# First mixer of a two-trunk transformer kernel: the order of attention and gated-recurrence work across steps, and the place of the modulation chunks in the load order

## The reference

```python
mix = concat([pool_mixer(p), gla_output(gla_bidir(...)), latent_attention(ql, k_all, v_all)]) @ w_out
x = x + ga1 * mix
x = x + ga2 * squared_relu_mlp(rmsnorm(x) * (1 + sc2) + sh2, w_up, w_down)
```

## Time and profile before

| | |
|---|---|
| median of 3 runs | 1920.18 us (1917.31 to 1926.2) |
| the profiled execution | 1921.07 us, its span 1919.3 us |
| PE busy | 1735.9 us, 90% |
| DVE busy | 1071.7 us, 56% |
| ACT busy | 704.2 us, 37% |
| mean granted PE clock | 0.942 |
| mixer of layer 0 | about 166.8 to 308.7 us from the start |
| mixer of layer 1 | about 847.1 to 936.5 us |

### The profile page before, as it was taken

How to read it: one execution, slowest core, us unless ns; L and a number is a source line. 1 busy time by engine, 2 the same in 40 slices (tenths; PEclk the granted TensorE clock), 3 DMA queues, 4 the chain that set the end, 5 groups by cost and what they waited for, 6 DMA issues and landing times.

```text
span 1919.3 us, 25681 instructions
## 1 busy us (share of the span) xinstructions
PE 1735.9 (90%) x10636; PEld 1399.4 (73%) x10636; DVE 1071.7 (56%) x1632; ACT 704.2 (37%) x878; POOL 81.6 (4%) x87
## 2 busy tenths in 40 slices
PE   5999888799999998988969996987999979779997
PEld 2886456677777777764669995675999766669996
DVE  2665545554444445764566775655666464566654
ACT  2423444321323123433444444363433343633332
POOL 0020000100000001100000001000000010010000
PEclk8999978899999999997889998988999989889999
DMA  9326860324344334258445555431654563335552
GB/s 340 117 103 218 284 224 1 134 87 151 133 150 149 140 132 145 94 208 313 169 143 201 190 180 170 178 132 45 197 176 165 180 225 122 122 110 176 176 174 90
DMA packets 172371, 309.18 MB, mean 161 GB/s; under 512 B 3264, under 2 KB 54720, under 8 KB 171616
## 3 DMA queue, kind: packets, MB, share of 16 engines
q1 hardware_dynamic: 168592, 293.98, 43.9%
q10 hardware_dynamic: 3376, 12.00, 1.8%
q0 software_dynamic: 288, 1.57, 0.2%
HBM read 305.44 MB, written 2.10 MB: 160 GB/s over the span
## 4 chain that ended last, share of the span: by engine, by line
PE 76%; DVE 11%; ACT 6%; DMA 4%; issue 2%; POOL 1%; DVEq 0%; ACTq 0%; POOLq 0%; SPq 0%
PE bank L581 58%; PE twin L581 15%; DVE ring_r L1230 3%; PE bank L590 3%; ACT arena L1961 2%; ACT arena_r L1961 2%; DMA ring<-in_w_in 2%; DMA ring<-in_w_mod 2%; DVE arena L1230 1%; POOL rs L2373 1%; DMA ring<-in_w_up 1%; DVE params L1230 1%; DVE arena L1314 1%; DVE arena_r L1230 1%; DVE X L1713 1%
## 5 line engine op out<-in xcount | busy, mean ns | idle before, releaser
L581 PE MATMUL bank<-arena_r 128*128 128x512 f32 (+2 forms) x2128 | 704.0, 377 | 15.4 <-DVE arena_r L1831 6.7
L1230 DVE TENSOR_TENSOR ring_r<-ring,arena_r 128x4096 fp32r<-128x4096 f32 (+4 forms) x96 | 393.9, 4103 | 236.2 <-ACT arena_r L1961 235.4
L581 PEld LDWEIGHTS bank<-arena_r 128*128 128x128 f32 x2128 | 406.6, 191 | 95.9 <-issue 8.0
L1961 ACT ACTIVATE arena_r<-ring 128x4096 fp32r<-128x4096 f32 (+4 forms) x96 | 323.4, 3369 | 393.9 <-DMA ring<-in_w_up 161.8
L581 PE MATMUL twin<-actT_r,arena_r 128*128 128x256 f32 x1408 | 255.3, 285 | 0.4 <-DVE actT_r L1230 0.4
L581 PE MATMUL bank<-ring_r,arena_r 128*128 128x512 f32 x624 | 246.7, 395 | 0.0
L581 PE MATMUL bank<-arena_r,actT_r 128*128 128x512 f32 (+3 forms) x624 | 219.5, 383 | 15.9 <-DVE params L1230 6.3
L581 PEld LDWEIGHTS twin<-actT_r,arena_r 128*128 128x128 f32 x1408 | 220.9, 193 | 1.0 <-DVE actT_r L1230 0.8
L1961 ACT ACTIVATE arena<-bank 128x512 f32<-128x512 f32 (+4 forms) x193 | 91.5, 474 | 343.6 <-PE bank L581 291.7
L581 PE MATMUL twin<-actT_r,ring_r 128*128 128x256 f32 x704 | 200.0, 284 | 0.0
L581 PE MATMUL bank<-ring_r,actT_r 128*128 128x512 f32 (+3 forms) x496 | 183.7, 370 | 0.0
(11 more groups left out here) (194 smaller groups left out, 1685.7 us busy)
## 6 DMA issues: line engine op xcount, KB each, us to landing
ring<-in_w_mod SPq DMA_DIRECT2D x24, 2048.0 KB, 8.8
ring<-in_w_ada SPq DMA_DIRECT2D x24, 2048.0 KB, 8.1
ring<-in_w_gate_up SPq DMA_DIRECT2D x44, 1024.0 KB, 7.7
ring<-in_w_down SPq DMA_DIRECT2D x20, 2048.0 KB, 8.0
ring<-in_w_up SPq DMA_DIRECT2D x16, 2048.0 KB, 7.9
ring<-in_w_in SPq DMA_DIRECT2D x12, 2048.0 KB, 9.2
ring<-in_w_out SPq DMA_DIRECT2D x8, 2048.0 KB, 8.6
ring<-in_w_down SPq DMA_DIRECT2D x8, 1792.0 KB, 7.5
```

Source lines behind the costliest of these rows:

```text
L581: ins = nc.tensor.matmul(out_, lhsT, rhs, start=start, stop=stop)
L1230: return v.tensor_tensor(o, x, y, op)
L1961: return nc.scalar.activation(o, x, func, **kw)
```

## The change

Load order: the last modulation chunk of each mixer moves ahead of out1 half 0, so the order is ..., mod, mod, out1 half 0, out1 half 1, up1 chunk 0, up1 chunk 1. Three places ahead of up1 chunk 0 now stands that modulation chunk, and three ahead of up1 chunk 1 stands out1 half 0.

Mixer: DVE takes the maxima of step i + 2 in step i instead of those of i + 1, and it does so behind `attended`, which now is for the pair that ended in step i - 2. PE makes its scores ahead of `turned1`. The parts of a gated tile are spread wider (PE: w, w + 1, w + 3, w + 5; DVE: w, w + 2, w + 4, w + 5). `WEIGHTED1` moves to 2, 6, 10, 14, so step w + 4 of a tile is step w of the next. ACT's block of gated exponentials is cut in two. The fills move up, all of them to the head of the step.

```diff
-        out += ins[:early] + [("par1", l, 0)] + ins[early:] + take(BESIDE1[l] - 1)
-        out += [("out1", l, 0)] + take(1) + [("out1", l, 1)]
+        out += ins[:early] + [("par1", l, 0)] + ins[early:] + take(BESIDE1[l])
+        out += [("out1", l, h) for h in range(2)]
...
-WEIGHTED1, FILLS1 = [[1, 6, 11, 16], [1, 7]], [(0, 1, 2, 3, 5, 6, 7, 9, 11, 12, 14, 16, 18, 20), (0, 1, 2, 4, 5, 6, 8, 9, 11, 13)]
-SUMS1, COLUMNS1, HALVES1 = [21, 7], [22, 13], [20, 12]
+WEIGHTED1 = [[2, 6, 10, 14], [2, 6]]
+FILLS1 = [(0, 1, 2, 3, 5, 6, 8, 9, 11, 12, 13, 15, 17, 19), (0, 1, 2, 4, 5, 6, 8, 9, 11, 13)]
+SUMS1, COLUMNS1, HALVES1 = [20, 7], [21, 13], [20, 12]
...
# PE
-                    if i in FILLS1[l] and i not in WEIGHTED1[l]:
+                    if i in FILLS1[l]:
                         fill()
+                    if i % 2 == 0 and i + 2 < n:
+                        scores1(l, i + 2)
                     if i < n:
                         turned1(l, i)
-                    if i % 2 == 0 and i + 2 < n:
-                        scores1(l, i + 2)
                     for p in ended(l, i - 1):
                         values1(l, p)
-                    if i in FILLS1[l] and i in WEIGHTED1[l]:
-                        fill()
                     for t in tiles:
                         w = WEIGHTED1[l][t]
-                        if i == w:
-                            if t + 1 in tiles:
-                                logs(l, t + 1)
+                        if i == w and t + 1 in tiles:
+                            logs(l, t + 1)
+                        if i == w + 1:
                             gated_scores(l, t)
-                        if i == w + 1:
+                        if i == w + 3:
                             gated_values(l, t)
-                        if i == w + 3:
+                        if i == w + 5:
                             gated_turned(l, t)
...
# DVE
                 largest1(l, 0)
+                largest1(l, 1)
                 differences(l, 0)
                 for i in range(n + 1):
-                    if i + 1 < n:
-                        largest1(l, i + 1)
+                    for p in ended(l, i - 2):
+                        attended(l, p)
+                    if i + 2 < n:
+                        largest1(l, i + 2)
+                    for p in ended(l, i):
+                        inverse_sums(l, p)
                     for t in tiles:
                         w = WEIGHTED1[l][t]
+                        if i == w + 2:
+                            masked(l, t)
+                        if i == w + 4:
+                            if t == 0:
+                                gate_values(l)
+                            gated_out(l, t)
+                        if i == w + 5:
+                            gated_norm(l, t)
                         if i == w:
                             ...
                             weighted(l, t)
-                        if i == w + 1:
-                            masked(l, t)
-                            if t + 1 in tiles:
-                                differences(l, t + 1)
-                        if i == w + 2:
-                            ...
-                            gated_out(l, t)
-                        if i == w + 3:
-                            gated_norm(l, t)
+                        if i == w + 1 and t + 1 in tiles:
+                            differences(l, t + 1)
                     if i == 2:
                         pooled(l)
...
-                    for p in ended(l, i - 1):
-                        attended(l, p)
+                    if i == n - 2:
+                        mixed_rest(l, range(0, 2))
                     if i == n - 1:
-                        mixed_rest(l, range(0, 4))
-                    if i == n:
-                        mixed_rest(l, range(4, 8))
+                        mixed_rest(l, range(2, 4))
+                for p in ended(l, n - 1):
+                    attended(l, p)
+                mixed_rest(l, range(4, 8))
...
# ACT
-            def exponents(l, t):
+            def exponents(l, t, part):
...
                 qk96, qk64, qk32, qd, kd = features(t)
-                step(f(qk96, qk96, ACT.Exp))
-                step(f(kd, qd, ACT.Exp, scale=-1.0))
-                step(f(qd, qd, ACT.Exp))
-                step(f(VIEWS1[l][4][t % 2], bT[:, :, :], ACT.Exp), exps_out)
+                if part == 0:
+                    act.wait_ge(exps_in, nth(exps_in))
+                    step(f(qk96, qk96, ACT.Exp))
+                else:
+                    step(f(kd, qd, ACT.Exp, scale=-1.0))
+                    step(f(qd, qd, ACT.Exp))
+                    step(f(VIEWS1[l][4][t % 2], bT[:, :, :], ACT.Exp), exps_out)
...
-                        if i == w + 1:
+                        if i == w + 1 and t + 1 in tiles:
+                            logs(l, t + 1)
+                        if i == w + 2:
                             main_scores(l, t)
-                            if t + 1 in tiles:
-                                logs(l, t + 1)
-                        if i == w + 4:
+                        if i == w + 6:
                             gated_turned(l, t)
...
                         if i == WEIGHTED1[l][t] + 2:
-                            exponents(l, t + 1)
+                            exponents(l, t + 1, 0)
+                        if i == WEIGHTED1[l][t] + 3:
+                            exponents(l, t + 1, 1)
...
+                    if i == n - 3:
+                        mixed_high(l, range(0, 2))
                     if i == n - 2:
-                        mixed_high(l, range(0, 4))
+                        mixed_high(l, range(2, 4))
```

More of the change, by code:

```diff
@@ L1563, in mixer1 @@
                             weighted(l, t)
-                        if i == w + 1:
-                            masked(l, t)
-                            if t + 1 in tiles:
-                                differences(l, t + 1)
-                        if i == w + 2:
-                            if t == 0:
-                                gate_values(l)
-                            gated_out(l, t)
-                        if i == w + 3:
-                            gated_norm(l, t)
+                        if i == w + 1 and t + 1 in tiles:
+                            differences(l, t + 1)
                     if i == 2:
@@ L1579, in mixer1 @@
                         split_part(("out1", l, 0), i - HALVES1[l] - 1)
-                    for p in ended(l, i):
-                        inverse_sums(l, p)
-                    for p in ended(l, i - 1):
-                        attended(l, p)
+                    if i == n - 2:
+                        mixed_rest(l, range(0, 2))
                     if i == n - 1:
-                        mixed_rest(l, range(0, 4))
-                    if i == n:
-                        mixed_rest(l, range(4, 8))
+                        mixed_rest(l, range(2, 4))
+                for p in ended(l, n - 1):
+                    attended(l, p)
+                mixed_rest(l, range(4, 8))
             def residual1(tiles, half, gates, behind=None, late=None):
@@ L2085, in logs @@
                 step(f(bT[:, :, :], b[:, :].rearrange("p (j n) -> p j n", j=4), ACT.Copy), a_emptied)
-            def exponents(l, t):
-                act.wait_ge(exps_in, nth(exps_in))
+            def exponents(l, t, part):
                 qk96, qk64, qk32, qd, kd = features(t)
-                step(f(qk96, qk96, ACT.Exp))
-                step(f(kd, qd, ACT.Exp, scale=-1.0))
-                step(f(qd, qd, ACT.Exp))
-                step(f(VIEWS1[l][4][t % 2], bT[:, :, :], ACT.Exp), exps_out)
+                if part == 0:
[5 more added lines that the diff above has]
+                    step(f(VIEWS1[l][4][t % 2], bT[:, :, :], ACT.Exp), exps_out)
             def main_scores(l, t):
@@ L2153, in mixer1 @@
                 exponents1(l, 0)
-                exponents(l, 0)
+                exponents(l, 0, 0)
+                exponents(l, 0, 1)
                 for i in range(n + 1):
```

## The result

| | median | runs |
|---|---|---|
| before | 1920.18 us | 1917.31 to 1926.2 (5) |
| after | 1932.11 us | 1931.74 to 1938.16 (5) |

The ratio is 1.0065, 95% interval [1.0042, 1.0088]: slower by 0.65%. The time lies 7.1 us above the forecast of 1925 and inside the range of 1908 to 1939. The forecast had the change (+4.9) within the 0.5% that can't be told from no change; it came out at +11.9, just beyond that line, though the interval reaches to 0.42%.

A forecast was written before the change was run, and what follows sets the result against it. PE bounds the kernel, losing time to waits in an order and clock dips. Gaps +16.0 and +10.9, last steps -2.2, clock -3, load order -16.8 sum to +4.9: 1926.0 profiled, median 1925 us, range 1908 to 1939.

The forecast's parts named there:

- Load order: Behind both mixers: the fetch of up1 chunk 0 leaves the chain after out1 half 0; -16.8 us.
- The gaps: PE idle in the mixers: 28.7 us for 12.7 in layer 0 (+16.0), 17.8 for 6.9 in layer 1 (+10.9).
- Step 2: PE's values wait for the bank of pooled, behind DVE's largest and weighted: gap 5.3 us in layer 0, 5.1 in layer 1.
- w + 2: Two steps after a gated tile's start, values wait for the bank masked empties: about 1.0 us each.
- w + 4 of t = 0: First gated tile: values wait for gated_out's first copy, with gate_values ahead: 3.35 us in layer 0, 2.3 in layer 1.
- Step 7: PE's gated_turned waits for DVE's gated_norm: gap 4.9 us in layer 0, 5.85 in layer 1.
- fills moved up never wait for their chunk: Mixer fills: a 2 MB chunk lands 6 to 8 us after its slot is read, so no wait was expected.
- The last steps: End of each mixer, set by ACT: copies a step earlier give 17.4 for 18.5 us, the like in layer 1; -2.2.
- The clock: PE's clock loss in the mixers: unchanged, but for work now hidden inside stretches that DVE sets; -3 us.
- Rival 1: Mixers: the long new gaps cost clock too, four more losses of 3.3 us; +13, 1938 us; chance 0.30.
- Rival 2: Mixers: the pipelining works, w + 5 gaps half as long and some clock back; 1909.7 us; chance 0.16.
- Rival 3: Load order: up1 chunk 0 isn't in place early, so the change doesn't do what it says; 1942 us; chance 0.04.

The follow-up runs named there:

- experiment 4: After, with zero-column products added to PE's list ahead of the waits of steps 2, 6, 7, 11, 15 (layer 1: step 2): 1922.61 us, ratio to before 1.0019.
- experiment 1: Before with only the new load order, the mixer untouched: 1900.97 us, ratio to before 0.9902.
- experiment 2: After with the old load order put back, so the new mixer alone: 1943.25 us, ratio to before 1.0132.
- experiment 7: After, with even-step maxima behind DVE's gated work and pooled, and gated_turned one step later on PE and ACT: 1875.37 us, ratio to before 0.9775.
- experiment 3: After, with DVE's maxima of even steps taken at the step's end, behind gated work and pooled: 1895.8 us, ratio to before 0.9878.

## Why the prediction was nearly right, and where it failed

**Load order: right.** -16.8 predicted; in the traces -10.0 (9 predicted) and -7.8 (7.8), alone on the chip -17.6.

**The gaps: right in kind, place and sum.** The layout gave 28.7 us for layer 0 up to step 20, the trace 141.30 - 115.00 = 26.3. Step 2: 5.3 for 5.34; w + 2: 1.0 for 1.01; w + 4 of t = 0: 3.35 for 3.34; steps 11, 15 and 19: 3.0, 4.0 and 0.8 for 2.75, 3.85 and 0.66. Two sizes were off. Step 7 was 3.40 for 4.9: the layout was made at full clock, and at full clock the wait is 4.82 (experiment 4), but in after PE ran the work ahead of it at half clock and came later. In layer 1, with PE at full clock there, it was 5.69 for 5.85. The later w + 4 gaps were 0.44 to 0.67 for 0.85, and the last w + 2 gap 0.57 for 1.0. Layer 1: 19.2 for 17.8, of which 1.64 is the wait that I had ruled out: "fills moved up never wait for their chunk" is wrong, for both layers have one in step 2 (0.82 and 1.64, ended by the modulation chunk).

**The last steps: no gain.** -2.2 predicted for both; 18.4 for 18.6 and 14.7 for 15.4 measured. ACT's list ends them, and with the same 68.6 us of work in the mixer, moving copies ahead changed little.

**The clock: the term that was mis-sized.** I took "unchanged", and then -3. In the profiled pair PE's busy time in the two mixers says +3.8 and -2.3, so +1.5. Idle time in the two whole mixers rose by 14.0 + 12.3 = 26.3, for +24.7 predicted (16.0 + 10.9 - 2.2). Together the mixers cost 27.8 us where 21.7 were predicted: 4.5 of the 6.1 are the clock, 1.6 the idle time. With a load order that gave 1.0 more than predicted, the touched stretches come to +10.0 for +4.9, and the medians differ by 11.9.

One pair of executions doesn't fix this term. Experiments 1 and 2 have the same two orders: there idle rises by 13.3 + 12.1, and busy time changes by -0.8 and +0.9. The mixers cost 25.5 us in these traces and 24.7 by the medians. "Unchanged" would have been right there, and the credit of 3 us for work inside the stretches that DVE sets shows in neither pair. The forecast of +4.9 is 7.0 short of one comparison and 2.2 short of the other, so how near it came is in part luck.

**Rival 1**, that the new order loses more clock than the old, isn't borne out as a difference: +1.5 in one pair, about 0 in the other, for its +13. It says "six" gaps of 3.8 us or longer where its own layout has five (5.3, 3.35 + 4.9, 4.0, 5.1, 5.85). Its mechanism, that gaps cost clock, is what experiment 4 shows: in layer 0 standing still cost 7 to 11 us of clock on top of the waits. The old order paid such a sum too, so the difference of the two hid it. I had priced the clock as a difference of two large losses and never asked what an order with few gaps would get back. In experiment 7 the two mixers have 16.9 us of idle time for 29.9 in experiment 1, and PE's own work in them takes 179.7 us for 197.9.

By the rule of the Trainium skill, "TensorE: Matmul & The Clock Gate", section "A second HAM failure mode: psum-queue depth-cycling", the clock term should have been above 0 rather than -3. The mean clock agrees in layer 0 (0.83 for 0.88 up to step 20). In layer 1 it depends on the execution of the old mixer: 0.88 for 0.84 in the profiled pair, 0.88 for 0.91 in experiments 2 and 1. But that mean counts the waits too, and the time that PE's own work took, +1.5 and about 0, shows hardly a difference. Between orders that differ more the rule's direction holds: 0.95 in layer 0 in the order with the fewest gaps.

**Rival 2**, that the pipelining works, is refuted for this order and true for a near neighbour: moving one wait (experiment 3) gave 1895.8, lower than its 1909.7. **Rival 3** is refuted: up1 chunk 0 was asked for early in both layers and the transfer left the chain.

**What stays open.** The profiled pair differs by 17.1 us, 10.0 in the touched stretches and 7.1 outside them (1.2 ahead of the first mixer, the rest behind), where no part of the change stands. By medians the difference is 11.9 us in the first comparison and 7.1 by the two parts; no run says why. Nor was it tried why the old mixer of layer 1 ran at 0.84 in before and 0.91 in experiment 1.

## What to carry to other kernels

Running ahead helps only if the operation that runs ahead waits for something from an earlier step. Put at the head of an in-order list with an input from this same step, it ties everything behind it to the other engine; at the end of the step the same call gave 30 to 36 us. And where a row shows TensorE's clock dipping, price an idle stretch at more than its length, and look for the order that has few of them; ask of each load what the chunk one ring length earlier still waits for, since a swap of two loads gave 17.6 us for nothing.

## What the runs showed of the hardware

- The clock loss depends on what PE does in a wait, not on the wait alone: zero-valued products in waits of 2.8 to 5.3 us gave a mean granted clock of 0.90 in the mixer, for 0.82 in after and 0.84 in experiment 2, and made it 10.3 and 5.0 us shorter, with the waits unchanged in sum (33.8 for 33.0 and 32.2). Products that aren't needed are thus a cheap test for this loss.
- In the ordinary matmuls the level can be read off single rows: the same 16 matmuls of `values1` take 1.09 us at full clock and 1.98 behind the gap of 5.34, the transposes of `gated_turned` 0.44 and 0.69. Such a pair behind one gap tells a reader that the clock is low before the clock's own row is looked up.
- The same gap in the same list can leave either level: behind step 6's wait, 3.34 us in after and 3.38 in experiment 2, those 16 matmuls took 1.98 and 1.09 us. In after PE was at half clock ahead of the gap too: the last fill before it took 3.64 us, in experiment 2 1.92. So two profiles of one mixer with such gaps differed by 4.5 us.
- In the execution of 5048.84 us PE was busy for 99% of the span, and the largest group of matmuls took 913 ns each where the other profile of that kernel has 376, at a granted clock that reads 1.00 throughout. The clock's row doesn't show every slow PE; what made this one is open.
